# First projection of a three-layer model: finer first transfers, a second issuing queue, rounding shared with VectorE

## The reference

```
n    = rmsnorm(h, g_mix[0])           # rows of x, each scaled by 1/rms and by a gain per column
proj = n @ w_in_ab[0]                 # 1024 x 3160; split into qa ka va | iq ik iw | qb kb vb g_low og
iq   = rope_partial(iq.reshape(1, 256, 8, 64), pos)     # the first columns that the kernel computes
ik   = rope_partial(ik[:, :, None, :], pos)[:, :, 0, :]
```

## Time and profile before

| what | value |
|---|---|
| median of 3 runs | 949.63 us |
| profiled execution | 949.28 us |
| its span from first to last instruction | 947.5 us |
| TensorE busy | 939.1 us |
| VectorE busy | 697.1 us |
| ScalarE busy | 594.3 us |

### The profile page before, as it was taken

The page is one execution under the profiler, slowest core; times in us unless marked ns, Lnnn a source line. Parts: engine busy times, 40 slices in busy tenths (PEclk is TensorE's granted clock), DMA queues, the critical chain, the costliest instruction groups (busy, mean ns, idle before and its releaser), DMA issues.

```text
span 947.5 us, 14533 instructions
## 1 busy us (share of the span) xinstructions
PE 939.1 (99%) x5956; PEld 834.9 (88%) x5956; DVE 697.1 (74%) x1006; ACT 594.3 (63%) x861; POOL 36.2 (4%) x15
## 2 busy tenths in 40 slices
PE   9999999999999999999999999999999999999997
PEld 7888888888888888888888888999999999999886
DVE  5997846777987667747787987676468699888643
ACT  7676548887644658748887654734555687655532
POOL 0021250000000000020000000000000000000000
PEclk9999999999999999999999999999999999999999
DMA  8654245555556452445555655354544435555541
GB/s 305 227 188 156 91 138 177 193 203 180 194 205 219 166 193 93 174 147 181 201 186 178 203 200 220 145 200 156 178 176 164 151 156 207 195 178 179 196 159 44
DMA packets 25345, 168.22 MB, mean 178 GB/s; under 512 B 2816, under 2 KB 3904, under 8 KB 5568
## 3 DMA queue, kind: packets, MB, share of 16 engines
q1 hardware_dynamic: 24848, 166.84, 49.3%
q10 hardware_dynamic: 432, 0.46, 0.1%
HBM read 166.24 MB, written 1.05 MB: 177 GB/s over the span
## 4 chain that ended last, share of the span: by engine, by line
PE 95%; DVE 2%; ACT 1%; issue 1%; POOL 0%; DVEq 0%; ACTq 0%; POOLq 0%
PE bank L709 23%; PE bank L710 23%; PE bank L711 23%; PE bank L818 12%; PE bank L822 6%; PE bank L737 1%; DVE wlo L1963 1%; PE bank L872 0%; PE bank L1091 0%; PE bank L1225 0%; PE bank L856 0%; ACT whi L1316 0%; PE bank L876 0%; PE bank L880 0%; PE bank L1117 0%
## 5 line engine op out<-in xcount | busy, mean ns | idle before, releaser
L1963 DVE TENSOR_TENSOR wlo<-raw,whi 128x2048 fp32r<-128x2048 f32 (+2 forms) x139 | 310.5, 2234 | 134.8 <-ACT whi L1316 134.6
L1316 ACT ACTIVATE whi<-raw 128x2048 fp32r<-128x2048 f32 (+1 forms) x142 | 270.3, 1905 | 69.4 <-PE bank L711 67.1
L818 PE MATMUL bank<-nhl,whi 128*128 128x512 f32 x512 | 124.2, 392 | 0.2 <-DVE nhl L1976 0.2
L818 PEld LDWEIGHTS bank<-nhl,whi 128*128 128x128 f32 x512 | 93.9, 188 | 19.4 <-issue 0.7
L709 PE MATMUL bank<-mhi,whi 128*128 128x258 f32 x384 | 108.6, 283 | 0.0
L710 PE MATMUL bank<-mlo,whi 128*128 128x258 f32 x384 | 108.3, 282 | 0.0
L711 PE MATMUL bank<-mhi,wlo 128*128 128x258 f32 x384 | 108.2, 282 | 0.0
L709 PE MATMUL bank<-nhl,whi 128*128 128x258 f32 (+3 forms) x320 | 92.3, 288 | 0.2 <-DVE nhl L1976 0.2
L710 PE MATMUL bank<-nhl,whi 128*128 128x258 f32 (+3 forms) x320 | 91.4, 286 | 0.0
L711 PE MATMUL bank<-nhl,wlo 128*128 128x258 f32 (+3 forms) x320 | 90.5, 283 | 0.0
L711 PEld LDWEIGHTS bank<-mhi,wlo 128*128 128x128 f32 x384 | 72.8, 189 | 0.0
(11 more groups left out here) (379 smaller groups left out, 1880.9 us busy)
## 6 DMA issues: line engine op xcount, KB each, us to landing
raw<-w_stream SPq DMA_DIRECT2D x154, 1024.0 KB, 4.8
h<-x_rows SPq DMA_DIRECT2D x4, 256.0 KB, 4.6
raw<-w_stream SPq DMA_DIRECT2D x2, 512.0 KB, 5.8
cst<-consts SPq DMA_DIRECT2D x1, 832.0 KB, 6.3
e<-g_post SPq DMA_DIRECT2D x1, 512.0 KB, 3.6
out_rows<-e SPq DMA_DIRECT2D x2, 256.0 KB, 2.0
raw<-w_stream SPq DMA_DIRECT2D x1, 352.0 KB, 9.2
vec<-vectors SPq DMA_DIRECT2D x1, 258.5 KB, 8.5
```

Source lines behind the costliest of these rows:

```text
L818: return pe.matmul(us[c].t[:, :], w[:, k, c * P:c * P + P].hi, nboth[:, k, :], start=k == 0, stop=k == 7)
L1316: act.activation(whi[j][:, 0:n], raw[j][:, 0:n], ACT.Copy).then_inc(s_hi.up(i))
L1963: dve.tensor_tensor(wlo[j][:, 0:m], raw[j][:, 0:m], whi[j][:, 0:m].bitcast(F32), ALU.subtract).then_inc(s_lod.up(i))
```

## The change

- SyncE sends x in three pieces a row tile (256, 256 and 512 columns) in place of two. Parts 2 and 3 of tile 0 go one by one between the second and the third piece, and tile 1 goes in two halves behind them.
- Parts 0 and 1 of tile 0 are issued from ScalarE's queue, behind the identity and ahead of its table load.
- VectorE rounds parts 0 and 1 (`hi00`, a copy) ahead of anything else. ScalarE rounds the other six.
- TensorE turns a quarter (two k, one bank) at a time: `first_turn`. 3 passes on zeros stand ahead of the first turn and 1 behind it. The second turn comes behind the first eight products, the third and fourth behind part 2.
- ScalarE squares the two row tiles at two separate places, rounds tiles 2 and 3 ahead of the row factors, and TensorE's two transposes of the factors move into the key products, ahead of k = 6.
- VectorE makes low part 2 ahead of its second evacuation; the other parts move along in the same way.

```diff
-                return [[(s_x[tt][c], 16) for c in range(2)] for tt in range(2)]
+                return [[(s_x[tt][c], 16) for c in range(3)] for tt in range(2)]
+        def hi01_ready(i, c):
+            return s_hi00.at(c) if i == 0 and c < 2 else s_hi01.at(i, c)
...
-            keep_warm(use["tr", 0, 2].t, AM[:, 0:P], AM[:, 0:256], 4)
-            half_turn(0, 0)
+            def first_turn(q):
+                u = begin("tr", 0, q)
+                on.wait_ge(*TI)
+                for tt in range(2):
+                    on.wait_ge(s_x[tt][min(q, 2)], 16)
+                    for kk in range(2):
+                        k = 2 * q + kk
+                        x = pe.transpose(u.t[:, kk * 256 + tt * P:kk * 256 + tt * P + P], h[:, tt, k * P:k * P + P], ident)
+                x.then_inc(u.full)
             keep_warm(use["tr", 0, 2].t, AM[:, 0:P], AM[:, 0:256], 3)
+            first_turn(0)
+            keep_warm(use["tr", 0, 2].t, AM[:, 0:P], AM[:, 0:256], 1)
...
+            def row_factors():
+                u = begin("rowf")
+                on.wait_ge(*s_stat.at(0, 1))
+                for tt in range(2):
+                    x = pe.transpose(u.t[:, tt * P:tt * P + P], bc(stats[0][2][:, tt:tt + 1], [P, P]), ident)
+                x.then_inc(u.full)
...
             for k in range(8):
+                if k == 6:
+                    row_factors()
                 x = mm3(u.t[0:88, 0:256], w[:, k, :], nTa[:, k, :], k == 0, k == 7)
...
             evac_turn(0, 0, nTa)
-            hi01(0, 0)
-            hi01(0, 1)
+            hi01(0, 2)
             evac_turn(0, 1, nTa)
+            hi01(0, 3)
+            row_squares(0, 0)
             evac_turn(0, 2, nTa)
-            hi01(0, 2)
-            hi01(0, 3)
-            evac_turn(0, 3, nTa)
             hi01(1, 0)
             hi01(1, 1)
+            evac_turn(0, 3, nTa)
             hi01(1, 2)
             hi01(1, 3)
-            row_stats(0)
+            hi(2)
+            row_squares(0, 1)
+            hi(3)
+            row_factors(0)
             rs = stats[0][2]
             on.wait_ge(*s_stat.at(0, 2))
-            hi(2)
-            hi(3)
...
+            def hi00(c):
+                s = slice(c * 512, c * 512 + 512)
+                on.wait_ge(*((s_w1, 16) if c else (s_raw[0], 16)))
+                dve.tensor_copy(whi[0][:, s], raw[0][:, s]).then_inc(s_hi00.up(c))
...
-            for c in range(2):
+            def rows_in(c, n0, n1):
                 for tt in range(2):
-                    sp.dma_start(h[:, tt, c * 512:c * 512 + 512], X[tt * P:tt * P + P, c * 512:c * 512 + 512]).then_inc(s_x[tt][c], 16)
-                sp.dma_start(raw[0][:, c * 1024:c * 1024 + 1024], first[:, c * 1024:c * 1024 + 1024]).then_inc(s_w if c else s_raw[0], 16)
-            for i in range(1, NSLOT):
+                    sp.dma_start(h[:, tt, n0:n1], X[tt * P:tt * P + P, n0:n1]).then_inc(s_x[tt][c], 16)
+            rows_in(0, 0, 256)
+            rows_in(1, 256, 512)
+            sp.dma_start(raw[0][:, 1024:1536], first[:, 1024:1536]).then_inc(s_w2, 16)
+            sp.dma_start(raw[0][:, 1536:2048], first[:, 1536:2048]).then_inc(s_w3, 16)
+            rows_in(2, 512, 1024)
+            sp.dma_start(raw[1][:, 0:1024], second[:, 0:1024]).then_inc(s_raw[1], 16)
+            sp.dma_start(raw[1][:, 1024:2048], second[:, 1024:2048]).then_inc(s_w67, 16)
+            for i in range(2, NSLOT):
                 stage(i)
...
             eng.dma_start(vec[:, o_id:NVEC], V[:, o_id:NVEC]).then_inc(s_i, 16)
+            first = W[0:starts[1]].rearrange("(p n) -> p n", p=P)
+            eng.dma_start(raw[0][:, 0:512], first[:, 0:512]).then_inc(s_raw[0], 16)
+            eng.dma_start(raw[0][:, 512:1024], first[:, 512:1024]).then_inc(s_w1, 16)
             scalar_program(eng)
```

More of the change, by code:

```diff
@@ L641, in block_kernel @@
         s_raw = [sem(f"raw{i}") for i in range(NSLOT)]
-        s_w, s_i, s_v, s_c, s_r, s_o, s_g, s_d, s_gp = (sem("s_" + n) for n in ("w", "i", "v", "c", "r", "o", "g", "d", "gp"))
-        s_x = [[sem(f"s_x{tt}{c}") for c in range(2)] for tt in range(2)]
+        s_i, s_v, s_c, s_r, s_o, s_g, s_d, s_gp = (sem("s_" + n) for n in ("i", "v", "c", "r", "o", "g", "d", "gp"))
+        s_x = [[sem(f"s_x{tt}{c}") for c in range(3)] for tt in range(2)]
+        s_w1, s_w2, s_w3, s_w67 = (sem("s_w" + n) for n in ("1", "2", "3", "67"))
         TI, TV, TC, TR, TM, TD, TGP = (s_i, 16), (s_v, 16), (s_c, 32), (s_r, 32), (s_g, 16), (s_d, 32), (s_gp, 16)
-        s_hi01, s_lo01 = sig("hi01", grid(2, 4)), sig("lo01", grid(2, 4))
+        s_hi00 = sig("hi00", range(2))
+        s_hi01, s_lo01 = sig("hi01", grid(2, 4)[2:]), sig("lo01", grid(2, 4))
         cuts = [cut(i) for i in range(NTILE)]
@@ L880, in low_weights @@
                     return pe.matmul(us[tt].t[:, :], nTa[:, k, tt * P:tt * P + P].hi, w[k // 4][:, k % 4, :].lo, start=False, stop=k == 7)
[L882 to L885, removed]
+                for part in (high, low_rows):
                     for k, tt in product(range(2), range(2)):
                         part(k, tt)
-                for k in range(2, 5):
-                    for part in (high, low_rows, low_weights):
+                first_turn(1)
+                for k, tt in product(range(2), range(2)):
+                    low_weights(k, tt)
+                for k in range(2, 6):
+                    for part in (high, low_weights, low_rows) if k == 2 else (high, low_rows, low_weights):
                         for tt in range(2):
@@ L893, in first_proj @@
                                 x.then_inc(us[tt].full)
-                for tt, k in product(range(2), range(5, 8)):
+                    if k == 2:
+                        first_turn(2)
+                        first_turn(3)
+                for tt, k in product(range(2), range(6, 8)):
                     high(k, tt)
@@ L1340, in hi01 @@
             def hi01(i, c):
-                on.wait_ge(*((s_w, 16) if i == 0 and c >= 2 else (s_raw[i], 16)))
+                on.wait_ge(*((s_w2, 16) if (i, c) == (0, 2) else (s_w3, 16) if i == 0 else (s_w67, 16) if c >= 2 else (s_raw[1], 16)))
                 act.activation(whi[i][:, c * 512:c * 512 + 512], raw[i][:, c * 512:c * 512 + 512], ACT.Copy).then_inc(s_hi01.up(i, c))
@@ L1355, in half_turn, with row_squares, row_factors @@
                     evac_turn(t, q, nTa if t < 4 else nT2[:, :, META:L2])
+            def row_squares(t, tt):
+                for r in h_ready(t)[tt]:
+                    on.wait_ge(*r)
+                act.activation(xn[:, tt, :], h[:, tt, :], ACT.Square, accum_out=stats[t][0][:, tt:tt + 1]).then_inc(own.up())
             def row_stats(t):
+                for tt in range(2):
+                    row_squares(t, tt)
+                row_factors(t)
+            def row_factors(t):
                 ss, lnrs, rs, rs2 = stats[t]
-                ready = h_ready(t)
-                for tt in range(2):
-                    for c in range(2):
-                        on.wait_ge(*ready[tt][c])
-                    act.activation(xn[:, tt, :], h[:, tt, :], ACT.Square, accum_out=ss[:, tt:tt + 1]).then_inc(own.up())
                 on.wait_ge(*own.last())
@@ L1998, in rope @@
                 dve.tensor_tensor(x2, tmp[2], tmp[3], ALU.add).then_inc(done.up(1))
+            hi00(0)
+            hi00(1)
             evac_turn(0, 0, nTa)
@@ L2802, in stage @@
                 sp.dma_start(raw[j][:, 0:n], src).then_inc(s_raw[j], 16)
-            first = W[0:starts[1]].rearrange("(p n) -> p n", p=P)
-            for c in range(2):
+            first, second = (W[starts[i]:starts[i + 1]].rearrange("(p n) -> p n", p=P) for i in range(2))
+            def rows_in(c, n0, n1):
                 for tt in range(2):
-                    sp.dma_start(h[:, tt, c * 512:c * 512 + 512], X[tt * P:tt * P + P, c * 512:c * 512 + 512]).then_inc(s_x[tt][c], 16)
-                sp.dma_start(raw[0][:, c * 1024:c * 1024 + 1024], first[:, c * 1024:c * 1024 + 1024]).then_inc(s_w if c else s_raw[0], 16)
-            for i in range(1, NSLOT):
+                    sp.dma_start(h[:, tt, n0:n1], X[tt * P:tt * P + P, n0:n1]).then_inc(s_x[tt][c], 16)
[7 more added lines that the diff above has]
+            for i in range(2, NSLOT):
                 stage(i)
```

15 lines of the change are left out of this document (5 added, 10 removed).

## The result

| kernel | median, us | lowest to highest | runs |
|---|---|---|---|
| before | 949.71 | 949.11 to 950.16 | 21 |
| changed | 950.76 | 949.84 to 952.64 | 21 |

The ratio is 1.0012, 95% interval 1.0007 to 1.0018. The changed kernel is slower by 1.05 us; the forecast was 0.4 us faster, with a range up to 950.4. Its runs also spread over 2.8 us where those of before spread over 1.05. The execution profiled here took 952.64 (span 950.7), the longest of the 21, and it shows one of two losses at its largest.

What follows compares the result with a forecast made beforehand. TensorE bound it, busy 939.1 of 947.5 us; only its wait before 7.46 could be won. A projection gain of 0.50 less 0.1 for close places gave 0.4 off 949.63: 949.2 us, range 948.3 to 950.4.

Steps and rivals of the forecast that it cites:

- Between these ends I take 6.3: Landing of weight part 1 from ScalarE's queue, taken as 6.3 us, between 5.8 and 6.8.
- both bounds: Part 1's landing: 6.8 us if the queues share evenly, 5.8 if ScalarE's queue gets two thirds.
- the bound of 6.8: Late end for part 1's landing: two queues share evenly, so it lands when 1161 KB have, at 6.8 us.
- the gain of 0.87 at the front: Second pair of products in the first projection starts at 7.12 in place of 7.99 us, 0.87 earlier.
- the four transposes that moved behind it: Four transposes, 0.11 us each, move from dead time before 7.46 into the busy stretch; 0.87 earlier becomes 0.50.
- the two close places: VectorE's first evacuation (needed by 8.0) and rounding of parts 4 and 5 (by about 13.3): 0.1 us charged together.
- rival (a): Part 1 gains nothing: landing 6.8 or later, second pair at 7.65, time 949.7 to 950.0 us; chance 0.27.
- TensorE behind TensorE: After the tile 3 and 4 waits, TensorE only follows itself, so what is won at the front stays won.
- Rival (c), the clock: Pauses at the start delay TensorE's rise from 1.2 to 2.4 GHz; 949.7 us and up, chance 0.10.
- a rise at 11.7: Late case of the clock loss: TensorE reaches 2.4 GHz only at 11.7 us, giving 951.5 us.
- The rounding: VectorE's copy of one 128x512 weight part, taken as 0.62 us from ScalarE's time; the skill's figure gave 0.33.
- The moved wait: Rounding tile 3 now precedes the row factors; low part ready 21.6, wanted 21.95: hidden, but gains over 0.85 cut.

Runs made afterwards that it cites:

- 950.24 run: The changed kernel executed once more with nothing altered, for a second trace: 950.24 us.
- 951.61 run: The changed kernel timed again in 11 runs with nothing altered, median 950.69 us; this is their profiled execution, 951.61 us.

## Why the prediction was wrong

**The step that failed** is "Between these ends I take 6.3", the landing of part 1. It landed at 7.4 (950.24 run) and 7.6 (952.64 run), outside both bounds. The even sharing behind the bound of 6.8 came out: 0.59 and 0.58 MB by then. What did not is the rate. Both bounds stretched the landed bytes of before, and with them the rate of before, over another set of transfers, and by 6.8 the engines had moved 1.17 MB in place of 1.42. Counting landed bytes hides how much moves: when the 1092.5 KB (1.12 MB) of before had landed, at 6.63, 1.37 MB had been sent, a part of it for later transfers. The first quarter of x's second tile failed in the same way: forecast for 4.2, it landed at 4.6 to 5.1 in four profiles, where twice its bytes took until 4.65 before.

What lowered the rate is shown in part. SyncE needs one slot of 0.45 us for each transfer (four in 1.80), and it now carries 128 KB where it carried 256. The run with two small issues shows the price of a slot (0.66 late in the queue, 0.96 late in landing), the two runs with two more transfers what such a cut costs the kernel (1.3 us). The second queue alone is not what lowers it. In the window of the fifth microsecond eight of the nine profiles with x's first half in transfers of 128 KB have 143 to 203 GB/s, among them four in which SyncE alone issues x and weights. The ninth, with the weights between the quarters, has 263, and halves of x with weight parts of 256 KB have 231. The eight with larger first transfers have 281 to 380, and the kernel before with weights on the second queue is one of these (303). In the changed kernel part 1 itself is issued on time, at 1.66, and in the 952.64 execution the DMA engines were busy for 0.79 of that window; why they deliver less there is not settled.

**What follows from it.** With the second pair at 7.98 in place of 7.12, the gain of 0.87 at the front is gone, and the four transposes that moved behind it remain: 0.44 was charged, with 0.1 for the two close places, and the projection ended 0.53 later than before (19.94, where the keys start, against 19.41). This part of the sum was right, and rival (a), "part 1 gains nothing", had the mechanism; its end of 949.7 to 950.0 was too low by a little, as the run at full clock took 950.24. Some 0.16 of this is not in the span at all, and the sum had no term for it: over 11 runs the changed kernel takes 1.96 us beyond its span, the kernel before 1.80 (33 runs), the changed kernel with the transfers of before 1.79. That everything behind tile 3 is "TensorE behind TensorE" holds: from its first product to the end of the span it is 924.7 to 925.4 us in all 18 profiles, so a loss at the front stays, and gains under some 0.7 us can't be read from single runs.

**Rival (c), the clock,** was real and had too small a chance, 0.10. Its counter-argument was that products come densely from 7.1 on. With the late landing TensorE stood still for 0.62 (950.24 run) and 0.85 (951.61 run) just ahead of the second pair, and in the second of these the granted clock then fell from 1.00 to 0.50. In the 952.64 execution the argument fails another way: products and transposes follow each other from 6.89 on, at 1.2 GHz and with at most 0.35 us between the two pairs, and the rise still came only at 13.5; why so late is not shown. For a rise at 11.7 the price was 951.5, so for 13.5, at 0.5 us each microsecond, 952.4. That is near 952.64, but it counts from a second pair at 7.12, which did not come; the firmer price is the 2.40 between two executions of the same kernel. By the medians with and without the full number of passes the clock is worth 0.4 to 0.5 us, the transfers about as much (0.53 from before to the run with all passes); the intervals overlap, so the split is rough. On the Trainium skill's rule that the prediction weighed ("TensorE: Matmul & The Clock Gate", Part 4: PE-mode transpose) the runs decide nothing: transposes and late data came together.

**The issuing queues.** The page "DMA: Bandwidth & Descriptors" of the Trainium skill (Issuing engines are not separate DMA queues) was on the right side with interleaving: the trace has both queues moving side by side, 0.59 and 0.58 MB by 6.8. It also says that the issue is usually small relative to the transfer; here two issues of 2 KB, 0.60 us together, moved the landing behind them by 0.96.

**The rounding** takes 0.43, not 0.62. The estimate from the Trainium skill's figure ("VectorE: DVE Perf Modes", The TRN2 errata) was 0.33; the same section says that this figure comes out too low for a single operation, and the trace agrees. The 0.2 won lies behind a transfer that is 1.1 late or more.

**The moved wait** is hidden in the changed kernel, as forecast: tile 3 follows the start of the keys by 3.03 and 3.04 in the two executions, as it did the end of the projection before (3.04). Where its data come late relative to the products, the wait appears as described: 0.2 and 0.7 us in the two runs with one queue.

## What to carry to other kernels

At the start of a kernel count the issues ahead of the data that the first product needs. In these runs each took its slot of 0.3 to 0.6 us in the queue, whether it carried 2 KB or 256, and every run that cut the first transfers finer made some of what stood behind them land later. Do not carry a landing rate over to another cut of the transfers: here 1.42 MB by 6.8 us became 1.17. Work that moves from dead time into the busy stretch costs its full length (four transposes, 0.44 us) unless the start really comes earlier. And one more pause of TensorE at the front can be paid for at half the clock (up to 2.40 us here).

## What was not expected

- Two transfers of 2 KB each cost 1.45 us of the whole kernel, about as much as cutting two transfers of 256 KB into four of 128 (1.3).
- From issue to landing the first weights took 4.2 to 6.3 us for 256 KB and 4.7 to 6.0 for 512 (the same 5.3 with issues at 1.64 and 2.29).
- TensorE fell to 1.2 GHz again after it had reached 2.4 (granted 0.73, then 0.50), in a kernel that is 99% busy, for some three microseconds.
- In the longest execution the clock column reads 1.00 throughout while the pitch of the products is that of 1.2 GHz: the pitch must be read beside it.
